# Matmul order within a k-tile: the 512-column products of both column tiles first, then both of 256

## The reference

```python
for i in range(DEPTH):                      # DEPTH = 2
    hn = rmsnorm(x, norm_mix[i])
    mix = mixer_ab(...) if i % 2 == 0 else mixer_c(...)
    x = x + mix
    hn = rmsnorm(x, norm_mlp[i])
    x = x + jnp.square(jax.nn.relu(hn @ mlp_w1[i])) @ mlp_w2[i]   # hidden width 8192
return rmsnorm(x, norm_final)
```

## Time and profile before

| | |
|---|---|
| median of three runs | 2278.11 us (2278.03 to 2278.43) |
| the profiled execution | 2278.34 us |
| its span, first to last instruction | 2276.6 us |
| mean granted TensorE clock | 0.995 |
| TensorE busy, matmuls | 2225.2 us (98%) |
| weight loads busy (they overlap matmuls) | 1961.4 us (86%) |
| VectorE, ScalarE, GpSimd busy | 1551.7, 1018.9, 166.2 us |
| DMA, mean rate | 184 GB/s |

### The profile page before, as it was taken

The page is one execution under the profiler, slowest core; times in us unless marked ns, Lnnn a source line. Parts: engine busy times, 40 slices in busy tenths (PEclk is TensorE's granted clock), DMA queues, the critical chain, the costliest instruction groups (busy, mean ns, idle before and its releaser), DMA issues.

```text
span 2276.6 us, 40505 instructions
## 1 busy us (share of the span) xinstructions
PE 2225.2 (98%) x14035; PEld 1961.4 (86%) x14035; DVE 1551.7 (68%) x2541; ACT 1018.9 (45%) x1465; POOL 166.2 (7%) x154
## 2 busy tenths in 40 slices
PE   6998979999999999999999999999999999999997
PEld 6997868888888888888888888888888888888886
DVE  7799367676576566567677777767756756766765
ACT  7620266544444444444454545444444444444442
POOL 1000002300000000000420000131000000000032
PEclk9999999999999999999999999999999999999999
DMA  8546555667657557567666565666666566566563
GB/s 229 167 124 153 139 185 157 189 190 206 188 185 210 189 187 210 187 191 202 187 196 186 176 189 170 185 186 186 192 185 184 191 196 189 189 192 187 184 194 111
DMA packets 438952, 418.00 MB, mean 184 GB/s; under 512 B 49627, under 2 KB 434859, under 8 KB 438348
## 3 DMA queue, kind: packets, MB, share of 16 engines
q1 hardware_dynamic: 435952, 414.30, 60.1%
q10 hardware_dynamic: 2908, 2.51, 0.4%
HBM read 406.35 MB, written 10.39 MB: 183 GB/s over the span
## 4 chain that ended last, share of the span: by engine, by line
PE 91%; DVE 6%; DMA 1%; ACT 1%; issue 0%; SPq 0%; DVEq 0%; ACTq 0%
PE psum L1579 54%; PE psum L1580 28%; PE psum L1576 2%; PE psum L1553 2%; DVE ysum L934 2%; PE psum L1755 1%; DVE whl L934 1%; DVE fa L934 1%; DVE wv L934 1%; DMA raw<-in_ab_w_in 1%; PE psum L1737 0%; DMA bias_a<-t_rel 0%; PE psum L1806 0%; PE psum L1732 0%; PE psum L1775 0%
## 5 line engine op out<-in xcount | busy, mean ns | idle before, releaser
L934 DVE TENSOR_TENSOR whl<-raw,whl 128x1024 fp32r<-128x1024 f32 x712 | 878.0, 1244 | 486.2 <-ACT whl L560 484.4
L560 ACT ACTIVATE whl<-raw 128x1024 fp32r<-128x1024 f32 x712 | 754.9, 1061 | 754.4 <-PE psum L1580 682.6
L1579 PE MATMUL psum<-act,whl 128*128 128x512 f32 x2560 | 892.5, 394 | 0.0
L1580 PE MATMUL psum<-act,whl 128*128 128x256 f32 x2560 | 713.6, 279 | 0.0
L1579 PE MATMUL psum<-hid,whl 128*128 128x512 f32 x2048 | 710.3, 392 | 0.0
L1579 PEld LDWEIGHTS psum<-act,whl 128*128 128x128 f32 x2560 | 479.7, 187 | 109.4
L1580 PE MATMUL psum<-hid,whl 128*128 128x256 f32 x2048 | 570.4, 279 | 0.0
L1580 PEld LDWEIGHTS psum<-act,whl 128*128 128x128 f32 x2560 | 482.3, 188 | 0.1
L1579 PEld LDWEIGHTS psum<-hid,whl 128*128 128x128 f32 x2048 | 383.5, 187 | 86.7
L1580 PEld LDWEIGHTS psum<-hid,whl 128*128 128x128 f32 x2048 | 385.7, 188 | 0.0
L571 ACT ACTIVATE half<-psum 128x256 f32<-128x256 f32 x344 | 113.7, 382 | 286.8 <-PE psum L1580 286.0
(11 more groups left out here) (201 smaller groups left out, 1789.9 us busy)
## 6 DMA issues: line engine op xcount, KB each, us to landing
raw<-in_mlp_w SPq DMA_DIRECT2D x512, 512.0 KB, 4.0
raw<-in_c_w_qkv SPq DMA_DIRECT2D x96, 512.0 KB, 4.6
raw<-in_ab_w_in SPq DMA_DIRECT2D x64, 512.0 KB, 4.2
raw<-in_ab_w_out SPq DMA_DIRECT2D x32, 512.0 KB, 4.4
raw<-in_c_w_out SPq DMA_DIRECT2D x32, 512.0 KB, 4.4
raw<-in_s_w_glu SPq DMA_DIRECT2D x8, 512.0 KB, 3.6
bias_c<-rpb_pad SPq DMA_DIRECT2D x64, 64.0 KB, 2.5
rpb_pad<-rpbw SPq DMA_DIRECT2D x4, 889.0 KB, 10.6
```

What stands on the lines that cost most here:

```text
L560: nc.scalar.activation(whl[:, s, :, 0, :], raw[:, s], ACT.Copy).then_inc(hi_done, 1)
L934: return nc.vector.tensor_tensor(dst, s0, s1, op)
L1579: pe.matmul(bank, *big, start=first, stop=False, skip_group_check=True)
L1580: last = pe.matmul(bank[:, 0:T], *little, start=False, stop=final, skip_group_check=True)
```

## The change

In `sub_mm` and in `glu_sub` the loop over the two column tiles becomes two loops: first both matmuls of 512 columns, then both of 256. The `joined` case gets a branch of its own ahead of that, with its order as before. The instructions, their operands, their number and the place of the semaphore's increment stay.

```diff
--- before.py
+++ after.py
@@ -1556,28 +1556,34 @@
                     ready(kt)
                     first, final = kt == 0, kt == KT - 1
                     tile = operand(kt)
+                    if joined:
+                        for n in range(2):
+                            cols = slice(n * P, (n + 1) * P)
+                            if token_major:
+                                w_hi, w_lo = whl[:, s, k, 0, :], whl[:, s, k, 1, :]
+                                parts = ((tile[:, 0, cols], w_hi), (tile[:, 0, cols], w_lo), (tile[:, 1, cols], w_hi))
+                            else:
+                                parts = ((whl[:, s, k, 0, cols], tile[:, 0, :]), (whl[:, s, k, 0, cols], tile[:, 1, :]),
+                                         (whl[:, s, k, 1, cols], tile[:, 0, :]))
+                            for c, (w, m) in enumerate(parts):
+                                last = pe.matmul(psum[:, banks + n, 0:T], w, m, start=(first and c == 0),
+                                                 stop=(final and c == 2), skip_group_check=True)
+                        continue
+
                     for n in range(2):
                         cols = slice(n * P, (n + 1) * P)
                         if token_major:
-                            w_hi, w_all = whl[:, s, k, 0, :], whl[:, s, k, :, :].rearrange("p h t -> p (h t)")
-                            big = (tile[:, 0, cols], w_all)
-                            little = (tile[:, 1, cols], w_hi)
+                            big = (tile[:, 0, cols], whl[:, s, k, :, :].rearrange("p h t -> p (h t)"))
                         else:
                             big = (whl[:, s, k, 0, cols], tile.rearrange("p h t -> p (h t)"))
+                        pe.matmul(psum[:, banks + n], *big, start=first, stop=False, skip_group_check=True)
+                    for n in range(2):
+                        cols = slice(n * P, (n + 1) * P)
+                        if token_major:
+                            little = (tile[:, 1, cols], whl[:, s, k, 0, :])
+                        else:
                             little = (whl[:, s, k, 1, cols], tile[:, 0, :])
-                        bank = psum[:, banks + n]
-                        if joined:
-                            w, m = big
-                            if token_major:
-                                parts = ((w, whl[:, s, k, 0, :]), (w, whl[:, s, k, 1, :]), little)
-                            else:
-                                parts = ((w, tile[:, 0, :]), (w, tile[:, 1, :]), little)
-                            for c, (w, m) in enumerate(parts):
-                                last = pe.matmul(bank[:, 0:T], w, m, start=(first and c == 0), stop=(final and c == 2),
-                                                 skip_group_check=True)
-                            continue
-                        pe.matmul(bank, *big, start=first, stop=False, skip_group_check=True)
-                        last = pe.matmul(bank[:, 0:T], *little, start=False, stop=final, skip_group_check=True)
+                        last = pe.matmul(psum[:, banks + n, 0:T], *little, start=False, stop=final, skip_group_check=True)
                 last.then_inc(subs_used, 1)
 
             def block_mm(i, j0, jb, operand, ready, token_major=False, joined=False, between=None):
@@ -1801,12 +1807,12 @@
                     kt = SUBK * (s % 2) + k
                     pe.wait_ge(y_split, kt + 1)
                     for n in range(2):
-                        cols = slice(n * P, (n + 1) * P)
-                        bank = psum[:, 2 * half_block + n]
-                        pe.matmul(bank, whl[:, s, k, 0, cols], act[:, NT + kt].rearrange("p h t -> p (h t)"),
-                                  start=(kt == 0), stop=False, skip_group_check=True)
-                        last = pe.matmul(bank[:, 0:T], whl[:, s, k, 1, cols], act[:, NT + kt, 0, :],
-                                         start=False, stop=(kt == NT - 1), skip_group_check=True)
+                        pe.matmul(psum[:, 2 * half_block + n], whl[:, s, k, 0, n * P:(n + 1) * P],
+                                  act[:, NT + kt].rearrange("p h t -> p (h t)"), start=(kt == 0), stop=False,
+                                  skip_group_check=True)
+                    for n in range(2):
+                        last = pe.matmul(psum[:, 2 * half_block + n, 0:T], whl[:, s, k, 1, n * P:(n + 1) * P],
+                                         act[:, NT + kt, 0, :], start=False, stop=(kt == NT - 1), skip_group_check=True)
                 last.then_inc(subs_used, 1)
 
             def v_sub(k):
```

## The result

| | before | after |
|---|---|---|
| median | 2277.73 us (20 runs, 2275.57 to 2282.32) | 2281.95 us (20 runs, 2279.75 to 2286.00) |
| ratio, 95% interval | | 1.0019 (1.0013 to 1.0025) |
| the profiled execution, its span | 2278.34, 2276.6 us | 2286.00, 2284.2 us |

The change costs about 4 us, clear of its interval. The profiled execution of after is the longest of its 20, so its excess of 7.7 us must not be read as the change's: 4.3 us of it had arisen before the first group of layer 0's output projection, in a part with few changed groups that also varied from profile to profile in the later runs (its end lay between 350.2 and 356.8 us). Of the later series, one run of before took 3696.79 us, at a granted clock of 0.557, and one of nudge 5122.97 us; the ratios leave both out.

The account below looks back on a forecast made before the run. TensorE, busy 98% of the span, was taken as the bound through the pitch of its matmul stream. Group steps 0 x 2720 and waits 0 us left the median of 2278.11 at 2278 us; range 2266 to 2310, the forecast's own 2274 to 2282.

Parts of the forecast that it names:

- part 4: Waits around each group and sub: none added, releases at the same place, no DMA moved; 0 us.
- (3): Steps within each group of four: 226.7 + 230 + 120 + 117 ns, by its reading exactly 693.3 as before; 0 us.
- Rival A: Every group: a 512 keeps 230 ns whoever follows, 256 before 256 costs 120; +10 us, 2288 us; 17%.
- Rival C: Stretches in the slow rhythm, up to 968 pairs: it goes as half the width changes go; 6 us faster, 2272; 17%.
- Rival B: The slow rhythm seen behind runs of 256s spreads to 4472 more pairs: +31 us, 2309 us; 14%.
- Rival D: Every group: the second of two 512s finds its weights loaded, starts after 216 ns; -29 us, 2249; 9%.
- The bank: Steps that leave a PSUM bank: no price, as eleven 256s in a row step by an even 120 ns.

Follow-up runs that it names:

- nudge: Kernel before plus a one-column fp32 matmul of zeros behind each run of exact products in layer 1: 2280.44 us, ratio 1.0010.
- runs8: Changed kernel, but a whole sub at a time, eight 512s and then eight 256s: 2292.28 us, 698.3 ns per group.
- hybrid: Changed kernel with the new order kept only in layer 1's attention projections and the gated unit: median 2283.36 us, ratio 1.0019 to before, in two groups of times.
- crossed: Changed kernel put back to alternating widths, but each 256 inside a block belongs to the other tile's bank: 2279.29 us, before 2276.59.
- bankswap: Changed kernel with the two 256s exchanged, so that 512 to 256 stays in its bank: 2284.51 us, before 2276.59.
- qkv_new: Changed kernel with the new order kept only in layer 1's input projections and the gated unit: 2274.66 us, ratio 0.9986 to before.
- block_more: As hybrid, with the first block of layer 1's MLP in the new order too: 2286.90 us, ratio 1.0015 to before.

## Why the prediction was wrong

*What bounds the kernel* was right: TensorE's pitch and nothing else; no wait, split or transfer moved (part 4 of the change).

*The forecast* said no change, and 1.0019 with an interval above 1 is a small but real loss. The measured 2281.95 lies at the very end of the forecast's own range, 2274 to 2282. The 4.2 us are even within the 4.6 that the prediction took for the limit of what can be told from no change; twenty runs of each kernel tell them apart. The step that failed is (3), "I take 226.7" for 512 to 512. The number is right for a stream that has settled, as runs8 shows (227 and 120), and so are the 13.3 ns over the bare columns at either width. (That the weight load costs them is not shown: every matmul here has a load of its own, also those of the earlier trace rows, which step by 0.215 us, some 2 ns over 512 column times.) What was wrong is to put settled prices on a group of four, which never settles. In it a 512 takes 233 ns, twice: 2 x 6.4 = 13 ns too much, and two 256s at 114.6 and 115.8 give 10 back. The forecast missed 3.3 ns per group and stood at zero. The fear that two 256s in a row leave no cover for their loads was not borne out: settled, they step by 120 ns, with the same 13.3 on top as a 512. That settled prices hold was the one thing that the earlier trace rows could not say, since each shows one rhythm only.

*Rival A* named the size, 697 ns per group, and the place, every group; measured 696.7. Its mechanism was wrong: a 512 does not keep 230 ns but takes 233, and the 256s take 115 and 116 instead of 120 and 117. That the sums agree is luck. And it was taken over all 2720 groups, +10 us, because A and C stood as alternatives. Both happened.

*Rival C*, the slow rhythm goes, was right as to place: the new order never showed 706.7 in its profile, not behind twelve 256s either. Its 6 us was too much: the stretches fall to 696.7, not to 693.3, and only some 840 of the 968 pairs were slow, since behind the transposes of line 1775 the old order runs at 693.3. The measured gain is 3.9 us, of which the output projection's part is there in some executions of before and in others not. Adding A on the two stretches outside (+7.4) and this gain gives the +3.5 of the profile.

*Rival B*, the slow rhythm spreads, did not happen to the new order. Hybrid shows that it is a real danger of the old one, and the term was sized well: 6.7 ns a pair, through a whole MLP.

*Rival D* is excluded: no 512 behind a 512 started after 216 ns; in the changed kernel's MLPs the step is never under 232, and the settled one is 227.

*The bank* was excluded in (3) from the earlier trace rows; crossed and bankswap show it.

## What to carry to other kernels

Where a matmul stream is the bound, a reordering of equal work is not free by default: ask of each step whether it was ever seen behind the same steps as in the order that is planned. The strict alternation in its good rhythm was the fastest here, runs of four of a width the slowest. A change made everywhere may mix a loss and a gain; split it by stage, and look at the single times as well as the median, since two groups of times tell of two rhythms.

## What the hardware showed that I had not expected

The float32r stream has memory: after 256-column matmuls at a settled 120 ns it takes five of 512 columns until the step is 227 ns, with 233, 236, 228, 233 and 231 on the way. The alternation of 512 and 256 has two steady rhythms at the same granted clock, 693.3 and 706.7 ns per four matmuls. In layer 1 it was slow behind each run of 256s, unless an inserted fp32 matmul stood between; at the norm, at the wait for `o_c` and where the old order follows the new one it went either way, and could then stay slow for an MLP's 700 us, which cost 13.7. No time of before or of qkv_new lies 13 us above the rest, and half of those of hybrid and block_more do, so the slow rhythm is not equally likely everywhere.

What state of the engine that is, these runs do not show: banks are out, and the extra over the bare columns is absent at 1.2 GHz; the rest is open. Nor is it settled why the MLP of layer 1 fell into the slow rhythm only where the output projection ahead of it ran in the new order.
